# Running key sums by group on VectorE, value halves side by side in one weight tile, and a new order of four engines in two attention layers

## The reference, cut to what matters

```
z = einsum('bhqd,bhkd->bhqk', qblk, kh) * scale
strict = kpos[None, :] < qp[:, None]
log_beta = log_sigmoid(z)
log_keep = where(strict, log_sigmoid(-z), 0)
between = cumsum(log_keep, over keys, reverse=True) - log_keep
w = where(strict, exp(log_beta + between), 0)
out = einsum('bhqk,bhkd->bhqd', w, vh)
```

## Time and profile before

| what | value |
|---|---|
| median of three runs | 2710.51 us |
| the profiled execution, whole | 2709.61 us |
| its span, first to last instruction | 2707.8 us |
| mean granted TensorE clock | 0.999 |
| TensorE (PE) busy | 2687.0 us, 99% |
| VectorE (DVE) busy | 1570.5 us, 58% |
| ScalarE (ACT) busy | 1153.1 us, 43% |
| GpSimd (POOL) busy | 625.6 us, 23% |

### The profile page before, as it was taken

The page is one execution under the profiler, slowest core; times in us unless marked ns, Lnnn a source line. Parts: engine busy times, 40 slices in busy tenths (PEclk is TensorE's granted clock), DMA queues, the critical chain, the costliest instruction groups (busy, mean ns, idle before and its releaser), DMA issues.

```text
span 2707.8 us, 31941 instructions
## 1 busy us (share of the span) xinstructions
PE 2687.0 (99%) x12902; PEld 2251.1 (83%) x12902; DVE 1570.5 (58%) x2312; ACT 1153.1 (43%) x1836; POOL 625.6 (23%) x401
## 2 busy tenths in 40 slices
PE   8999999999999999999999999999999999999999
PEld 7888888888888888888888888888888887888887
DVE  7556555344566646665575668744545668755444
ACT  4323423222347636532236767522224667622223
POOL 1000111011136525400004642411102452411100
PEclk9999999999999999999999999999999999999999
DMA  4222232332221222223222221233333221232332
GB/s 163 99 97 93 97 102 93 101 99 96 90 80 56 72 70 67 86 98 101 97 94 92 82 63 40 80 100 100 95 96 101 78 62 49 71 101 94 97 98 78
DMA packets 69412, 238.78 MB, mean 88 GB/s; under 512 B 7696, under 2 KB 10256, under 8 KB 69264
## 3 DMA queue, kind: packets, MB, share of 16 engines
q1 hardware_dynamic: 69264, 236.73, 27.1%
HBM read 234.60 MB, written 2.10 MB: 87 GB/s over the span
## 4 chain that ended last, share of the span: by engine, by line
PE 93%; DVE 3%; ACT 2%; issue 0%; DMA 0%; POOL 0%; SPq 0%; ACTq 0%; DVEq 0%
PE ps L416 30%; PE ps L418 29%; PE ps L417 29%; PE ps L552 1%; DVE ptl L1644 1%; PE ps L777 1%; PE ps L776 1%; PE ps L485 0%; ACT wh L1018 0%; PE ps L612 0%; PE ps L613 0%; PE ps L452 0%; PE ps L476 0%; ACT pth L1027 0%; PE ps L471 0%
## 5 line engine op out<-in xcount | busy, mean ns | idle before, releaser
L1018 ACT ACTIVATE wh<-raw 128x1024 fp32r<-128x1024 f32 (+2 forms) x453 | 465.0, 1028 | 728.1 <-PE ps L418 724.0
L416 PE MATMUL ps<-xh,wh 128*128 128x512 f32 x1920 | 751.9, 392 | 0.0
L417 PE MATMUL ps<-xl,wh 128*128 128x512 f32 x1920 | 747.7, 389 | 0.0
L418 PE MATMUL ps<-xh,wl 128*128 128x512 f32 x1920 | 747.6, 389 | 0.0
L1636 DVE TENSOR_TENSOR wl<-raw,wh 128x1024 fp32r<-128x1024 f32 (+1 forms) x339 | 449.9, 1328 | 147.0 <-ACT wh L1018 146.6
L416 PE MATMUL ps<-yh,wh 128*128 128x512 f32 x1088 | 425.0, 391 | 1.0 <-ACT ob L1419 0.8
L416 PEld LDWEIGHTS ps<-xh,wh 128*128 128x128 f32 x1920 | 360.7, 188 | 75.5 <-issue 1.2
L417 PE MATMUL ps<-yl,wh 128*128 128x512 f32 x1088 | 423.4, 389 | 0.0
L418 PE MATMUL ps<-yh,wl 128*128 128x512 f32 x1088 | 423.4, 389 | 0.0
L418 PEld LDWEIGHTS ps<-xh,wl 128*128 128x128 f32 x1920 | 360.7, 188 | 75.3
L417 PEld LDWEIGHTS ps<-xl,wh 128*128 128x128 f32 x1920 | 360.8, 188 | 75.0 <-issue 1.0
(11 more groups left out here) (267 smaller groups left out, 3630.7 us busy)
## 6 DMA issues: line engine op xcount, KB each, us to landing
raw<-in_ff SPq DMA_DIRECT2D x120, 512.0 KB, 3.6
raw<-in_pool_in SPq DMA_DIRECT2D x64, 512.0 KB, 3.3
raw<-in_conv_in SPq DMA_DIRECT2D x64, 512.0 KB, 3.2
raw<-in_pool_out SPq DMA_DIRECT2D x32, 512.0 KB, 3.2
raw<-in_qk SPq DMA_DIRECT2D x32, 512.0 KB, 3.6
raw<-in_pool_grp SPq DMA_DIRECT2D x16, 512.0 KB, 3.2
raw<-in_conv_out SPq DMA_DIRECT2D x16, 512.0 KB, 3.3
raw<-in_mla_z SPq DMA_DIRECT2D x16, 512.0 KB, 3.6
```

The lines of the kernel that those rows point to most:

```text
L416: pe.do.matmul(o, lh, rh_, start=start, stop=False)
L417: pe.do.matmul(o, lh, rl_, start=False, stop=False)
L418: return pe.do.matmul(o, ll, rh_, start=False, stop=stop)
L1018: act.do.activation(h[:, 0:ncol], r[:, 0:ncol], ACT.Copy).then_inc(*mark("whi", ("whi", k)))
```

## The change

There are three parts.

Running sums by group. After `kept` of a group, VectorE adds to block kb, from its column 128 on, the block kb+1 behind it, in place in SA. Since the groups come in the order 2 and 3, 1, 0, block kb then holds the sum of all blocks from kb on. `sb_between` needs two stationary matrices per block only: `trir` on block kb, and its complement `restr` on block kb+1. It has 14 matmuls in place of 20.

```diff
+                        kb = kbs[0]
+                        if kb < 2:
+                            dve.wait_ge(*at("kept", l, h, kb + 1))
+                        a = SA[:, KOFF[kb] + 128:KOFF[kb] + 512 - 128 * kb]
+                        dve.wait_ge(*mine())
+                        dve.do.tensor_tensor(a, a, SA[:, KOFF[kb + 1]:KOFF[kb + 1] + 384 - 128 * kb], ALU.add).then_inc(
+                            *mark("dve", ("kept", l, h, kb)))
...
-                            for jb in range(kb, 4):
-                                lhs = trir if jb == kb else onesr
+                            for jb in range(kb, min(kb + 2, 4)):
+                                lhs = trir if jb == kb else restr
```

```diff
+                    for kb in range(4):
+                        cc = slice(KOFF[kb], KOFF[kb] + 512 - 128 * kb)
+                        v = VS[0][2 * kb + h // 4][:, h % 4 * 128:h % 4 * 128 + 128]
+                        pe.do.matmul(b[:, kb * 128:512], v, SBH[:, cc], start=kb == 0, stop=False)
+                        mm = pe.do.matmul(b[:, kb * 128:512], v, SBL[:, cc], start=False, stop=kb == 3)
...
+                def sb_tail(h):
...
+                    high(YL[p][64 * e:64 * e + 64, :], ps("pv", l, "s", h)[64:128, :], ("mm", "pv", l, "s", h),
+                         ("pvtail", l, h))
...
+                def sb_sum(h):
...
+                    dve.do.tensor_tensor(b[0:64, :], b[0:64, :], f(YL[p][64 * e:64 * e + 64, :]), ALU.add).then_inc(
+                        *mark("dve", ("pvsum", l, h)))
...
-                    low(YL[p][rr, :], ps("pv", l, "s", h)[rr, :], YH[p][rr, :], ("yh", "wo", l, p, e),
+                    low(YL[p][rr, :], ps("pv", l, "s", h)[0:64, :], YH[p][rr, :], ("yh", "wo", l, p, e),
```

```diff
-                df_scores(3, 34)
                 sb_scores(5)
+                df_scores(3, 34)
...
-                wo(1, 1, (2,))
-                wo(1, 4, (0, 1, 2))
-                wo(1, 3, (0, 1, 2))
-                sb_pv(7)
+                wo(1, 3, (0, 1, 2))
+                wo(1, 4, (0, 1, 2))
+                sb_pv(7)
+                wo(1, 1, (2,))
+                wo(1, 2, (2,))
                 wo(1, 0, (2,))
```

More of the change, by code:

```diff
@@ L1399, in df_exp @@
                         act.wait_ge(*at("mm", "tp", l, h - 1, 2))
+                    elif l == 0:
+                        for m in range(8):
+                            act.wait_ge(*at("x", 4, m))
                     blocks = []
@@ L1494, in second_layer @@
                 turned("dq", 3)
-                keep(3)
+                keep(3, 0)
+                taking('sk', l, 2)
+                keep(3, 1)
+                sb_tail(2)
                 rot("dq", 2)
-                taking('sk', l, 2)
                 sb_out(2)
                 df_high(0)
+                keep(3, 2)
+                plain("sk", 2)
+                taking('dk', l, 3)
+                df_turn(1)
+                plain("sq", 2)
                 taking('sq', l, 2)
-                plain("sk", 2)
+                df_exp(2, 34)
@@ L2205, in second_layer @@
+                keep(0, 2)
+                turned("dq", 0)
+                rot("dq", 0)
+                between(0, 2)
+                between(0, 0)
+                between(0, 1)
+                turned("dk", 0)
                 v_low(0, 1)
-                rot("dq", 0)
-                between(0)
-                turned("dk", 0)
-                weights_of(0)
                 rot("dk", 0)
+                weights_of(0, 1)
+                weights_of(0, 0)
+                weights_of(0, 2)
@@ L2211, in second_layer @@
                 project("sq", 1)
+                df_max(0, 34)
+                soft(1, 0)
+                soft(1, 1)
+                soft(1, 2)
+                keep(1, 0)
+                keep(1, 1)
                 plain("sq", 1)
-                df_max(0, 34)
-                soft(1)
-                keep(1)
-                sb_out(0)
+                keep(1, 2)
+                sb_sum(0)
                 turned("dk", 1)
                 project("sk", 1)
-                between(1)
+                sb_out(0)
@@ L2266, in second_layer @@
+                soft(4, 0)
+                soft(4, 1)
+                soft(4, 2)
                 df_sums(2)
                 df_join(2)
+                keep(4, 2)
+                df_norm(1)
                 turned("dk", 3)
-                keep(4)
+                keep(4, 0)
+                keep(4, 1)
                 project("sq", 3)
                 df_turn(2)
-                df_norm(1)
+                between(4, 1)
+                between(4, 2)
+                between(4, 0)
                 rot("dk", 3)
-                between(4)
+                sb_sum(3)
```

524 lines of the change are left out of this document (323 added, 201 removed).

## The result

The changed kernel takes 2721.45 us (median of 5 runs, 2720.1 to 2725.4) against 2710.51 us for the kernel before: a ratio of 1.0043, 95% interval 1.0031 to 1.0054. It is 0.4% slower; 2694 us, 0.6% faster, was predicted. The profiled execution has a span of 2718.3 us against 2707.8, 10.5 us longer.

What follows compares the result with a forecast made beforehand. TensorE's instruction stream was taken as the bound, busy 2687.0 of 2707.8 us. 2709.6 - 19.7 + 2 x 0.9 + 2 x 0.6 = 2692.9, plus 0.9 for the median: 2694 us, 8-in-10 range 2687 to 2703.

Steps and rivals of the forecast that it cites:

- The stream: TensorE, `sb_between` and `sb_pv`: 160 matmuls fewer save 9.3 and 10.4 us, 19.7 us over 16 heads.
- the forecast's own charges of 3.0 us: TensorE waits added back in the sum: 2 x 0.9 us at head 4 and 2 x 0.6 us at the tail.
- Head 6 can take 1.25 us. Head 7 would lose 0.6 us a layer ... I take the two as equal: 0: Last group of `sb_between`: head 7's loss offset by ScalarE's earlier next step; net 0, bad end 0.6 us a layer.
- The other five have more than head 6: Last group of `sb_between`: the remaining five heads have more slack than head 6's 1.76 us for `keep`'s low parts.
- The moved work: GpSimd scales x4 and x1 before a second-projection weight tile, 2.8 us; charged 0, with 1.5 us as bad end.
- Head 4: Stretch where VectorE sets the pace: TensorE's 1.2 us saving lost, less 0.3; charged 0.9 us a layer, ends 0 and 3.
- rival B: New order also removes old waits at `df_scores` (L797) and L776, and forecast losses do not come: 2688 us; chance 0.15.
- Rival A: VectorE's stretch at head 4 grows beside GpSimd's tiles, head 7's additions are late: about 2700 us; chance 0.27.
- The tail: Behind `sb_pv(7)`: 2.9 us chain under 2.1 us cover, wait 0.8 instead of 0.2; 0.6 us a layer.
- The additions: VectorE: three a head on 128, 256 and 384 columns, 0.28, 0.42 and 0.55 us, 1.25 us a head.
- the surcharge of 6 us: VectorE additions with both inputs in SBUF held by GpSimd: 0.13 us on each of 48, nearly all under cover.
- Rival C: Slower: held additions delay `keep`'s low parts 4.5 us at heads 4, 6 and 7; 2716 us; chance 0.04.

Runs made afterwards that it cites:

- guard: Changed kernel with four GpSimd weight tiles of each layer made to wait until the VectorE low parts beside them are done; 2697.24 us.
- guard_plain: Changed kernel's order lists and banks with four GpSimd tiles a layer held back, but without running sums and without value halves side by side; 2712.4 us.
- order_new: Kernel before with only the changed kernel's new order lists and PSUM banks: no additions, no tail copy, no sum; 2721.7 us.
- guard_more: guard with the tile of wo(1,1) also held until head 6's weights' low parts are done, and sq,2's scaling ahead of sk,2's low part; 2702.0 us.
- filled: Changed kernel with 66 (first layer) and 30 (second) extra 128-column matmuls ahead of `sb_pv(0)`'s waits, not altering the result; 2724.8 us.
- filled_wide: Changed kernel with 18 and 10 extra 512-column matmuls ahead of `sb_pv(0)`'s waits, and 3 ahead of the first `df_scores(0, 34)`; 2719.3 us.

## Why the prediction was wrong

- **The stream, -19.7 us: right.** 160 matmuls fewer; 2.08 us for `sb_between(0)` against 2.1 forecast, 1.21 us for `sb_pv(7)` against 1.3. Where tiles are held back at the four places (guard against guard_plain) 15.2 us of it reach the end, and the forecast's own charges of 3.0 us leave 16.7. guard's 2697 us comes near the forecast of 2694, with a treatment that the forecast did not have. The first head's `sb_pv` was forecast at 1.3 us and took 2.38, at half the clock.
- **The step that failed: "Head 6 can take 1.25 us. Head 7 would lose 0.6 us a layer ... I take the two as equal: 0", and with it "The other five have more than head 6".** The bullets charge 1.5 us a layer for waits; the runs show 21.0 us of long waits in the two layers. The slack was read from one execution of before, for the kept low parts only and not for those of the weights, and only VectorE's added work was set against it. Where the new lists put a low part against a GpSimd tile was not looked at, though the order of both engines' instructions is known without a run. Head 7's low parts ended at 1709.29 us in before and the GpSimd tile began at 1709.45; head 0's ended at 1519.2 and the tile began at 1519.5. In the changed kernel `v_low(0, 1)` and `rot("dk", 0)` stand between `between(0)` and head 0's low parts, so that these begin 0.4 us before the tile. 4.9 us of slack (1524.14 against 1519.20) became 4.53 us of waiting. The two rows of the trace of before that show the near miss, the last two low parts of head 0's weights and the tile:

```profile
1517.33 1.87 DVE L1644 TENSOR_TENSOR ptl<-s,pth 128x384 fp32r<-128x384 f32 x2 [0.34 <-ACT pth L1027]
...
1519.51 5.19 POOL L2417 TENSOR_TENSOR wl<-raw,wh 128x1024 fp32r<-128x1024 f32 x2 [1.36 <-ACT wh L1018]
```

- **What the list left out: the clock.** No step of the prediction mentions it. Half clock rose from 3.4 to 23.9 us, worth some 7 us; 8.7 us is what the page's busy times leave for it and for anything else that makes a matmul longer.
- **"The moved work: 0": not shown wrong.** TensorE waited for no weight tile of GpSimd, and the tile beside head 0's weights began when ScalarE's rounding released it (2.00 us of idle time before it), not when the scalings ended. But the bullet asks only who waits for GpSimd's tiles; what counted is who is held by them.
- **Head 4, 0.9 us a layer: too dear.** The three waits around it sum to 1.5 us in the first layer (0.40, 0.46 and 0.65), in before to 2.0 (0.28, 1.35 and 0.41); the 1.35 us at `df_scores`, which rival B saw go, are gone. TensorE came there later by its waits at head 0 and at `df_turn(1)`, though, so the bullet was not tried under its own conditions. Rival A named this stretch as the danger; it is not where the time went.
- **The tail, 0.8 us of waiting: 0.72 us measured** at the part on row chunk 3.
- **The additions: right in sum.** They have means of 349, 431 and 865 ns for 128, 256 and 384 columns, 16 of each: 26.3 us against 20 forecast without holds and 26 with the surcharge of 6 us. The 384-column ones were forecast at 550 ns and are the held ones, which was a sign of being wrong. TensorE's long waits end on none of them, but they stand ahead of the low parts on which they end: the entry at `sb_between` is 8.2 us here and 4.1 in order_new, which has no additions, and which TensorE runs with more matmuls. How much of the difference is theirs is not shown.
- **Rival C, chance 0.04, was the one that came.** Its mechanism (a hold of up to 3.3 us) and its sign were right, its places only in part: it put the hold at heads 4, 6 and 7, and the largest was at head 0's weights. It also laid it to held additions, where the long waits end on low parts. That its 24.8 us of delays come near the 21.0 of long waits is luck: at the kept low parts of heads 4, 6 and 7, for which it said 10.6 us a layer, the first layer has 4.1. Its 2716 us lacked the clock. The chance rested on "GpSimd is busy 109 of 248 us", a mean share, where the question was four instants.

## What to carry to other kernels

Before an order of instructions is changed, list for each pair of engines that hold each other which long instruction will run beside which short one that somebody waits for; slack measured under the old order says nothing of it. A wait that keeps an idle engine's long instruction back for a few us costs nothing if its result is not wanted yet; four of them a layer were worth more here (24 us) than 160 matmuls. Which instruction it will run beside instead has to be looked up too: in guard_more the hold only moved on. And a saving in a stream that is 99% busy can be lost again to the clock, by short stands whose effect could not be told from their length here.

## What the runs showed of the hardware

- A VectorE instruction with two SBUF inputs beside a GpSimd weight tile: three low parts in 5.96 us against 1.62 us alone, one of 512 columns in 2.84 against 0.69. The low parts from PSUM beside the same tiles were not stretched (0.68 us at 1623.62 us, within the tiles of 1619.74).
- The granted clock fell to 1.2 GHz at 1523.8 us right behind a stand of only 0.46 us, which followed 64-row products and transposes. In guard a stand of 0.44 us at the same place did not bring it down. 66 matmuls of 128 columns behind the fall, with TensorE shown busy, did not bring it back (17.1 us at the low level in filled); with 512-column matmuls there and in the short stand ahead it stayed at 2.4 GHz (filled_wide).
- guard_more: shorter waits at `df_turn(1)` (1.0 to 0.4 us) and `sb_pv(0)` (0.67 to 0.19), TensorE idle for 26.8 us against guard's 26.6, and 10 us more at half clock. The clock's share of a change does not follow from the length of the waits.
